# Second mixer of a two-block network: rotary partners moved by transfers and GpSimd, and its score work in another order

## The chip, the cores and the metric

The kernel runs on one core of one Trainium2 chip. The metric is device time in microseconds of one execution; the median of three runs of the kernel before is 993.6 us (989.09 to 994.18). Five engines run their own instruction lists and meet at semaphores: TensorE (PE; its weight loads are PEld), VectorE (DVE), ScalarE (ACT), GpSimd (POOL) and SyncE (SP), which here only issues transfers. All data is float32; a product of weights and activations is made from a rounded upper part and a remainder (`whi`, `wlo`), so each weight block has to be split before it is used.

## The reference, cut to what matters

Two transformer-like blocks run one after the other on 256 tokens of width 1024. The change touches the mixer of the second block only:

```python
proj = h @ w_in[l]                      # 1024 -> 2304 columns, 18 groups of 128
qa, ka, va, qd, kd, vd = jnp.split(proj, splits, axis=-1)
qa = apply_rope(qa, cos, sin)           # 8 heads of 64; likewise ka (2), qd (8), kd (8)
# apply_rope: x1, x2 = halves of a head's 64 columns
#   [x1 * c - x2 * s, x2 * c + x1 * s]
out_a = sliding_window_sink_attention(qa, ka, va, sinks[l])      # "swa"
od = differential_attention(qd, kd, vd, lam)    # softmax(0) - lam * softmax(1), times vd
out_b = rms_norm_2(od, g_diff[l]) * (1.0 - lam_init)
x = x + jnp.concatenate([out_a, out_b], axis=-1) @ w_out[l]
```

## The kernel before, in words

Weights come in units of 128 x 1024 numbers (512 KB). SP loads a unit into one of three `raw` buffers, ACT rounds it into `whi` (L1179) and DVE subtracts to get `wlo` (L1694), both rings of six. `load` waits for the `wlo` of the unit three before (`lo_ready`), and both splits wait until PE has used the unit six before (`unit_used`). `split_to(i + LEAD + 1)` at the head of each step of ACT's and DVE's loops keeps the splits four units ahead of PE.

The mixer's projection is 18 units, one group of 128 columns each, in the order `COLS2`; PE makes a unit with 24 matmuls (`a_unit_summed`) in PSUM bank 4, 5 or 6 in turn. Columns lie on partitions, so a head's two rotary halves are two quarters of 32 partitions. For a rotated group (13 of the 18: groups 0 to 4 and 6 to 13) ACT copies the four quarters crosswise out of PSUM (L1532, four instructions), DVE multiplies the bank by the cosines (`RT[0]`, L2248, which frees the bank: `q_sum`), the swapped copy by the sines (L2249), and adds (L2252: `rope_done`). Value groups (5 and 14 to 17) are copied (L2242), turned by PE (L1000) and evacuated by ACT (L1546).

The twelve jobs of the softmax are numbered by `ORDER`: 0 to 5 belong to the differential heads, 6 to 11 to swa. `scores(p)` on PE makes jobs 2p and 2p+1, at a fixed place between units. `maxima(k)` (DVE L2194, then L2204 or L2197 and two small ones) masks and takes maxima, `exponents(k)` (ACT L1512) follows, `invert_sums(k)` (DVE) divides; for each pair of differential jobs it also subtracts the second map (L2222, L2227: `p_ready`). `turn(k)` on PE transposes a group of four blocks (L980), `turned(k)` on ACT evacuates it (L1521). Nine such groups exist: 0 to 2 differential, 3 to 8 swa.

After the units PE multiplies the differential maps by the values. ACT then squares the result and takes a root (L1559, L1564), DVE inverts and scales (L2269, L2272), PE transposes (L1047), ACT and DVE write the product's two parts (L1569, L1739), and the output projection starts on them: 8 units of the `w_out` loop, the first four on the differential half. Between those run the swa product (48 matmuls of 128x64), its scaling, and its transposes (L1077); the last four output units follow. The order is all written out by hand; no scheduler changes it.

## Time and profile before

| what | us |
|---|---|
| median of three runs | 993.6 |
| lowest, highest | 989.09, 994.18 |
| the profiled execution's own time | 990.36 |
| its span in the profile | 988.6 |
| mixer, first projection unit to first product of the differential maps | 614.69 to 683.68 |
| from there to the first output unit | 683.68 to 694.84 |
| from there to the fifth output unit | 694.84 to 715.36 |
| busy over the span: PE, DVE, ACT, POOL | 939.6, 663.3, 557.0, 20.8 |

The start times are those of the first matmul of each part in PE's timeline. A matmul's end is modelled, so PE's busy share overstates how much of the time it needs; how long a piece of work takes is better read as the difference between two start times. Idle time of an engine counts only where PE waits for it in the end.

### The profile page before, as it was taken

What the parts mean: (1) busy time and instruction counts of PE and PEld (TensorE: products, weight loads), DVE (VectorE), ACT (ScalarE), POOL (GpSimd) and SP (SyncE); (2) the same over time, 40 slices, a digit from 0 to 9 for tenths busy, and PEclk for the clock granted to TensorE, in tenths of its full rate; (3) what the DMA queues carried; (4) which work ended last, traced back from release to release, by engine and by line L of the source; (5) the groups of instructions that cost most, each with busy time, mean ns of one, the idle gap of its engine ahead of it and who ended that gap; (6) DMA issues with size and microseconds to landing.
All of it is one profiled execution on the core that took longest, in us unless ns stands there. A gap on an engine that the chain in (4) does not pass through costs nothing. (4 is left out here: it accounts for less than half of the span.)

```text
span 988.6 us, 17818 instructions
## 1 busy us (share of the span) xinstructions
PE 939.6 (95%) x6292; PEld 811.4 (82%) x6292; DVE 663.3 (67%) x1097; ACT 557.0 (56%) x1018; POOL 20.8 (2%) x47
## 2 busy tenths in 40 slices
PE   6999999989989999999999999987888999999997
PEld 5788888889989877888888887977777888888885
DVE  4776666567776467766667886788367366666665
ACT  6565555477545337555555676887566346454442
POOL 3002000000000001000000000000000000000000
PEclk9999999999999999999999999999999999999999
DMA  7677666545210226765666665542156236665652
GB/s 216 204 223 222 205 183 186 164 128 151 86 66 4 65 88 166 214 187 185 186 184 198 198 174 167 171 127 88 43 149 192 61 116 197 189 202 172 198 182 85
DMA packets 204241, 153.75 MB, mean 156 GB/s; under 512 B 5323, under 2 KB 189872, under 8 KB 204192
## 3 DMA queue, kind: packets, MB, share of 16 engines
q1 hardware_dynamic: 202896, 151.08, 50.7%
q0 software_dynamic: 1296, 2.01, 0.9%
q8 instruction: 32, 0.52, 0.2%
q14 instruction: 17, 0.14, 0.0%
HBM read 152.02 MB, written 1.05 MB: 155 GB/s over the span
## 5 line engine op out<-in xcount | busy, mean ns | idle before, releaser
L474 PE MATMUL ps<-XT,whi 128*128 128x512 f32 (+1 forms) x1728 | 521.1, 363 | 7.1 <-DVE XT L1739 7.1
L1694 DVE TENSOR_TENSOR wlo<-raw,whi 128x1024 fp32r<-128x1024 f32 x280 | 336.6, 1221 | 105.8 <-ACT whi L1179 82.6
L474 PE MATMUL ps<-XT,wlo 128*128 128x256 f32 x1440 | 405.6, 282 | 0.0
L474 PEld LDWEIGHTS ps<-XT,whi 128*128 128x128 f32 x1728 | 307.5, 190 | 64.2 <-issue 7.6
L1179 ACT ACTIVATE whi<-raw 128x1024 fp32r<-128x1024 f32 x280 | 291.8, 1054 | 52.3 <-PE ps L474 12.2
L474 PEld LDWEIGHTS ps<-XT,wlo 128*128 128x128 f32 x1440 | 273.9, 190 | 2.8
L474 PE MATMUL ps<-whi,H 128*128 128x512 f32 x608 | 177.7, 393 | 1.9 <-issue 1.6
L474 PEld LDWEIGHTS ps<-whi,H 128*128 128x128 f32 x608 | 108.9, 188 | 25.0 <-issue 1.8
L474 PE MATMUL ps<-wlo,H 128*128 128x512 f32 x304 | 95.6, 392 | 0.0
L474 PE MATMUL ps<-arena 64*64 64x64 f32 (+6 forms) x1512 | 87.9, 245 | 6.3 <-ACT arena L1374 1.7
L474 PEld LDWEIGHTS ps<-arena 64*64 64x64 f32 (+3 forms) x1512 | 80.3, 150 | 13.0 <-issue 2.3
L474 PEld LDWEIGHTS ps<-wlo,H 128*128 128x128 f32 x304 | 57.1, 188 | 13.3
L474 PE MATMUL ps<-whi,XT 128*128 128x512 f32 x192 | 56.9, 401 | 1.5 <-DVE XT L1738 0.8
L1241 ACT ACTIVATE arena<-ps 128x256 f32<-128x256 f32 x44 | 16.7, 380 | 57.6 <-PE ps L474 57.6
L1251 ACT ACTIVATE arena<-ps 128x256 f32<-128x256 f32 x44 | 16.9, 383 | 50.6 <-PE ps L474 50.6
L474 PEld LDWEIGHTS ps<-whi,XT 128*128 128x128 f32 x192 | 35.2, 188 | 10.5 <-issue 2.5
L1259 ACT ACTIVATE H<-arena 128x256 fp32r<-128x256 f32 x44 | 18.4, 418 | 38.5 <-DVE arena L1839 38.5
L1635 ACT ACTIVATE arena<-ps 128x256 f32<-128x256 f32 x32 | 12.2, 382 | 46.8 <-PE ps L474 46.7
L1828 DVE TENSOR_TENSOR arena<-ps,arena 128x256 f32<-128x256 f32 x44 | 18.6, 422 | 27.6 <-ACT arena L1241 27.5
L1842 DVE TENSOR_TENSOR H<-arena,H 128x256 fp32r<-128x256 f32 x44 | 18.7, 426 | 24.4 <-ACT H L1259 24.4
L1639 ACT ACTIVATE H<-arena 128x256 fp32r<-128x256 f32 x32 | 13.4, 418 | 35.0 <-DVE arena L2357 35.0
L1739 DVE SCALAR_TENSOR_TENSOR XT<-ps,VEC,XT 128x256 fp32r<-128x256 f32 x60 | 24.3, 475 | 10.6 <-ACT XT L1216 6.9
(259 smaller groups left out, 704.3 us busy)
## 6 DMA issues: line engine op xcount, KB each, us to landing
raw<-in_ffn_w_gate SPq DMA_DIRECT2D x44, 512.0 KB, 4.3
raw<-in_ffn_w_up SPq DMA_DIRECT2D x44, 512.0 KB, 3.7
raw<-in_ffn_w_down SPq DMA_DIRECT2D x44, 512.0 KB, 4.5
raw<-in_w_in SPq DMA_DIRECT2D x36, 512.0 KB, 3.8
raw<-in_w_up SPq DMA_DIRECT2D x32, 512.0 KB, 4.0
raw<-in_w_down SPq DMA_DIRECT2D x32, 512.0 KB, 4.5
raw<-in_w_out SPq DMA_DIRECT2D x16, 512.0 KB, 3.5
raw<-in_w_ckv SPq DMA_DIRECT2D x16, 512.0 KB, 4.4
```

The source lines that it names most:

```text
L474: return pe.matmul(o, st, mv, start=start, stop=stop, skip_group_check=True)
L1179: act.activation(whi[:, n % RING, :], raw[:, n % RAW, :], ACT.Copy).then_inc(hi_ready, 1)
L1241: act.activation(GL[:, q, :], PS[4 + q][:, T:2 * T], ACT.Copy).then_inc(g_low, 1)
L1251: act.activation(UL[:, q, :], PS[6 + q][:, T:2 * T], ACT.Copy).then_inc(u_low, 1)
L1259: act.activation(H[:, q, 0:T], HS[:, q, :], ACT.Copy).then_inc(h_hi, 1)
L1635: act.activation(UL[:, q, :], PS[4 + q][:, T:2 * T], ACT.Copy).then_inc(r_low, 1)
L1639: act.activation(H[:, q, 0:T], HS[:, q, :], ACT.Copy).then_inc(r_hi, 1)
L1694: dve.tensor_tensor(wlo[:, n % RING, :], raw[:, n % RAW, :], whi[:, n % RING, :].bitcast(F32), sub).then_inc(lo_ready, 1)
L1739: return dve.scalar_tensor_tensor(XT[:, c, T:2 * T], ps, scale, hi, mul, sub)
L1828: dve.tensor_tensor(GS[:, q, :], PS[4 + q][:, 0:T], GL[:, q, :], add).then_inc(g_raw, 1)
L1842: dve.tensor_tensor(H[:, q, T:2 * T], HS[:, q, :], H[:, q, 0:T].bitcast(F32), sub).then_inc(h_ready, 1)
```

## The change

1. Rotary partners. ACT copies the bank once, unswapped (`QCP`). SP then issues four transfers of 32 x 256 numbers (32 KB each) that write the quarters crosswise into `SWP`, in a new function `partners`, called ahead of the load eight units on. DVE keeps the cosine product alone. GpSimd makes the sine product and the sum (`RSW` lies in `LWG`).
2. Order of the units: the differential heads' query and key groups are interleaved and come first, then their values, then swa's key, its queries, its values.
3. The score work: `scores(0)` to `scores(3)` stand after units 5, 9, 10 and 16 (before: 7, 9, 11, 13), `scores(4)` and `scores(5)` behind the differential product; maxima, exponents, inversions and turns are placed by tables. The swa turns 3 to 8 now stand between the output units 0 to 3, two ahead of each of the units 1 and 2 and two behind unit 2.
4. PSUM banks are given out anew to fit.

```diff
--- before.py
+++ after.py
@@ -272,6 +272,8 @@
         SWP = CLOW
+        QCP = ar(24064, 2, T)
+        RSW = LWG[:, 0:T]
...
@@ -366,7 +369,7 @@
-        VALUES = (13, 14, 15, 16, 17)
+        VALUES = (8, 9, 10, 11, 17)
@@ -377,9 +380,15 @@
         ORDER = [6, 7, 8, 9, 10, 11, 0, 2, 1, 3, 4, 5]
-        COLS2 = [6, 7, 8, 9, 10, 11, 12, 13, 0, 1, 2, 3, 4, 5, 14, 15, 16, 17]
+        COLS2 = [6, 10, 7, 11, 8, 12, 9, 13, 14, 15, 16, 17, 4, 0, 1, 2, 3, 5]
+        ROPED = [i for i, k in enumerate(COLS2) if k < 5 or 6 <= k < 14]
         OUT2_ROWS = (4, 5, 6, 7, 0, 1, 2, 3)
-        U_BANKS, TURN_BANKS = (4, 5, 6), (7, 7, 7, 3, 3, 4, 5, 4, 5)
+        U_BANKS, TURN_BANKS = (4, 5, 6), (7, 7, 7, 4, 5, 6, 7, 4, 5)
+        SC_BANKS = (0, 1, 2, 0, 1, 2, 0, 1, 4, 5, 6, 7)
+        SCORES_AT, TURN_AT = {5: (0,), 9: (1,), 10: (2,), 16: (3,)}, {10: 0, 14: 1, 16: 2}
+        MAX_AT = {5: 0, 6: 1, 9: 2, 10: 3, 11: 4, 12: 5, 16: 6, 17: 7}
...
+        INVERT_AT = {7: 0, 8: 1, 11: 2, 12: 3, 13: 4, 14: 5}
@@ -440,10 +449,24 @@
+            def partners(i):
...
+                r = ROPED.index(i)
+                sp.wait_ge(q_copy, r + 1)
+                if r >= 2:
+                    sp.wait_ge(rope_sin, r - 1)
+                for a, b in ((0, 1), (1, 0), (2, 3), (3, 2)):
+                    sp.dma_start(SWP[QUADRANTS[a], r % 2, :], QCP[QUADRANTS[b], r % 2, :]).then_inc(swp_in[r % 2], 16)
             for i, k in enumerate(COLS2):
+                partners(i - LEAD - RAW - 1)
                 load(B_WIN2 + i, 0, cols("w_in_2", k * P))
             for i, c in enumerate(OUT2_ROWS):
+                partners(N_WIN2 + i - LEAD - RAW - 1)
                 load(B_WOUT2 + i, 0, rows("w_out_2")[:, c:c + 1, :])
+            partners(N_WIN2 + KC - LEAD - RAW - 1)
@@ -941,9 +964,14 @@
-                    for k in (2 * p, 2 * p + 1):
-                        if k >= 3:
-                            pe.wait_ge(sc_sum, k - 2)
+                    if p in (1, 2):
+                        pe.wait_ge(sc_sum, 2 * p - 1)
+                    elif p == 3:
+                        pe.wait_ge(sc_sum, 5)
+                    elif p == 4:
+                        pe.wait_ge(q_sum, N_WIN2)
+                    elif p == 5:
+                        pe.wait_ge(vt_ev, 5)
...
@@ -969,12 +997,10 @@
                         pe.wait_ge(sc_exp, 6 + k - 3 + 1)
-                        if k == 3:
-                            pe.wait_ge(vt_ev, 5)
-                        elif k in (5, 6):
-                            pe.wait_ge(od_norm, k - 4)
+                        if k < 7:
+                            pe.wait_ge(sc_sum, 6 + k)
                         else:
-                            pe.wait_ge(pt_ev, k if k == 4 else k - 1)
+                            pe.wait_ge(pt_ev, k - 3)
@@ -985,52 +1011,17 @@
+                def turn_value(i, n, bank):
+                    pe.wait_ge(q_sum, i + 1)
+                    for tt in range(NT):
+                        last = pe.transpose(PS[bank][:, tt * P:(tt + 1) * P], QKV[:, COLS2[i], tt * P:(tt + 1) * P], ident)
+                    last.then_inc(vt_mm, 1)
...
-                    if i == 7:
-                        pe.wait_ge(rope_done, 6)
-                        scores(0)
-                    if i == 9:
-                        pe.wait_ge(rope_done, 8)
-                        scores(1)
-                    if i == 11:
-                        scores(2)
-                    if i == 13:
-                        pe.wait_ge(rope_done, 13)
-                        pe.wait_ge(ksw_ready, 1)
-                        scores(3)
-                    if i in (15, 17):
-                        scores(i // 2 - 3)
-                    if i in (12, 14, 16):
-                        turn(i // 2 - 6)
...
+                for i in range(N_WIN2):
+                    if i >= 3:
+                        pe.wait_ge(q_sum, i - 2)
+                    a_unit_summed(B_WIN2 + i, PS[U_BANKS[i % 3]], None if i else "mix2")
+                    if i - 1 in VALUES:
+                        n = VALUES.index(i - 1)
+                        if n:
+                            pe.wait_ge(vt_ev, n)
+                        turn_value(i - 1, n, 3)
+                    if i in SCORES_AT:
+                        pe.wait_ge(rope_done, {5: 4, 9: 8, 10: 8, 16: 11}[i])
+                        if i == 16:
+                            pe.wait_ge(ksw_ready, 1)
+                        scores(SCORES_AT[i][0])
+                    if i in TURN_AT:
+                        turn(TURN_AT[i])
...
+                pe.wait_ge(sc_sum, 6)
+                pe.wait_ge(vt_ev, 4)
+                pe.wait_ge(pt_ev, 3)
+                diff_out(0)
+                turn_value(N_WIN2 - 1, 4, 7)
+                diff_out(1)
+                pe.wait_ge(rope_done, 13)
+                scores(4)
+                scores(5)
...
+                pe.wait_ge(sc_sum, 8)
+                output(0, start=True)
+                turn(3)
+                turn(4)
+                output(1)
                 turn(5)
                 turn(6)
-                pe.wait_ge(sc_sum, 12)
-                pe.wait_ge(pt_ev, 5)
-                output(0, start=True)
+                output(2)
                 turn(7)
                 turn(8)
-                output(1)
-                output(2)
@@ -1520,61 +1546,68 @@
...
-                        if i not in VALUES:
-                            act.wait_ge(unit_used, B_WIN2 + i + 1)
-                            if n_rope >= 2:
-                                act.wait_ge(rope_done, n_rope - 1)
-                            for a, b in ((0, 1), (1, 0), (2, 3), (3, 2)):
-                                ins = act.activation(SWP[QUADRANTS[a], n_rope % 2, :],
-                                                     PS[U_BANKS[i % 3]][QUADRANTS[b], 0:T], ACT.Copy)
-                            ins.then_inc(q_swap, 1)
...
+                for i in range(N_WIN2):
+                    split_to(B_WIN2 + i + LEAD + 1)
+                    if i in ROPED:
+                        r = ROPED.index(i)
+                        act.wait_ge(unit_used, B_WIN2 + i + 1)
+                        if r >= 2:
+                            act.wait_ge(swp_in[r % 2], 64 * (r // 2))
+                        act.activation(QCP[:, r % 2, :], PS[U_BANKS[i % 3]][:, 0:T], ACT.Copy).then_inc(q_copy, 1)
...
+                squares(0)
+                value_turned(N_WIN2 - 1, 4, 7)
+                squares(1)
                 act.wait_ge(od_ss, 2)
                 act.activation(ODS, ODS, ACT.Sqrt, scale=1.0 / P, bias=con("eps_block")).then_inc(od_std, 1)
-                turned(3)
-                turned(4)
+                exponents(7)
                 for h in range(4):
...
+                exponents(8)
+                exponents(9)
+                turned(3)
+                turned(4)
                 exponents(10)
                 exponents(11)
-                for k in range(5, 9):
-                    turned(k)
+                turned(5)
+                turned(6)
                 split_to(B_WOUT2 + RING)
+                turned(7)
+                turned(8)
@@ -2241,42 +2273,38 @@
...
-                        dve.wait_ge(q_swap, n_rope + 1)
-                        dve.wait_ge(own_dve, own.n)
-                        if n_rope:
-                            dve.wait_ge(rope_done, n_rope)
-                        dve.tensor_tensor(RT[:, 0, :], bank[:, 0:T], RC, mul).then_inc(q_sum, 1)
-                        dve.tensor_tensor(RT[:, 1, :], SWP[:, n_rope % 2, :], RSN, mul).then_inc(own_dve, own.next())
-                        dve.wait_ge(q_sum, i + 1)
-                        dve.wait_ge(own_dve, own.n)
-                        dve.tensor_tensor(QKV[:, k, :], RT[:, 0, :], RT[:, 1, :], add).then_inc(rope_done, 1)
-                        n_rope += 1
+                        r = ROPED.index(i)
+                        dve.wait_ge(q_copy, r + 1)
+                        if r == 0:
+                            dve.wait_ge(own_dve, own.n)
+                        if r >= 2:
+                            dve.wait_ge(rope_done, r - 1)
+                        dve.tensor_tensor(RT[:, r % 2, :], bank[:, 0:T], RC, mul).then_inc(q_sum, 1)
...
-                    if i >= 8:
-                        maxima(i - 8)
-                    if i >= 10:
-                        invert_sums(i - 10)
-                maxima(10)
-                invert_sums(8)
-                maxima(11)
-                invert_sums(9)
+                    if i in MAX_AT:
+                        maxima(MAX_AT[i])
+                    if i in INVERT_AT:
+                        invert_sums(INVERT_AT[i])
+                maxima(8)
...
-                invert_sums(10)
-                invert_sums(11)
+                for k in range(9, 12):
+                    maxima(k)
+                for k in range(6, 12):
+                    invert_sums(k)
@@ -2442,6 +2470,15 @@
+            for r, i in enumerate(ROPED):
+                pool.wait_ge(swp_in[r % 2], 64 * (r // 2 + 1))
+                pool.wait_ge(q_sum, i + 1)
+                if r:
+                    pool.wait_ge(rope_done, r)
+                pool.tensor_tensor(RSW, SWP[:, r % 2, :], RSN, ALU.mult).then_inc(rope_sin, 1)
+                pool.wait_ge(rope_sin, r + 1)
+                pool.tensor_tensor(QKV[:, COLS2[i], :], RT[:, r % 2, :], RSW, ALU.add).then_inc(rope_done, 1)
```

DVE at the projection units 7 and 8, before (units 5 and 6 read like unit 7; `arena` is the buffer in which `RT`, `SWP`, `QKV` and the scores lie; each L2248 stands for one rotated unit):

```order
L1694 TENSOR_TENSOR wlo<-raw,whi 128x1024 [waits unit_used,hi_ready]
L2248 TENSOR_TENSOR arena<-ps,arena 128x256 [waits rope_done,own_dve,q_swap]
L2249 TENSOR_TENSOR arena<-arena 128x256
L2252 TENSOR_TENSOR arena<-arena 128x256 [waits own_dve,q_sum]
L1694 TENSOR_TENSOR wlo<-raw,whi 128x1024 [waits unit_used,hi_ready]
L2248 TENSOR_TENSOR arena<-ps,arena 128x256 [waits rope_done,own_dve,q_swap]
L2249 TENSOR_TENSOR arena<-arena 128x256
L2252 TENSOR_TENSOR arena<-arena 128x256 [waits own_dve,q_sum]
L2194 SCALAR_TENSOR_TENSOR arena<-ps,CON 128x512 [waits sc_mm]
L2204 TENSOR_REDUCE arena<-arena 128x2 [waits sc_sum]
```

DVE at units 5 and 6 now, the first two with scores:

```order
L1727 TENSOR_TENSOR wlo<-raw,whi 128x1024 [waits unit_used,hi_ready]
L2282 TENSOR_TENSOR arena<-ps,arena 128x256 [waits rope_done,q_copy]
L2227 SCALAR_TENSOR_TENSOR arena<-ps,CON 128x512 [waits sc_mm]
L2237 TENSOR_REDUCE arena<-arena 128x2 [waits sc_sum]
L1727 TENSOR_TENSOR wlo<-raw,whi 128x1024 [waits unit_used,hi_ready]
L2282 TENSOR_TENSOR arena<-ps,arena 128x256 [waits rope_done,q_copy]
L2227 SCALAR_TENSOR_TENSOR arena<-ps,CON 128x512 [waits sc_mm]
L2237 TENSOR_REDUCE arena<-arena 128x2 [waits sc_sum]
L1727 TENSOR_TENSOR wlo<-raw,whi 128x1024 [waits unit_used,hi_ready]
```

L2282 is the cosine product that was L2248; the two instructions behind it are gone, and the scores' maxima (L2227, L2237) stand in the steps of units 5 and 6 and no longer in those of 8 and 9.

What took their place stands on GpSimd's list, once per rotated unit:

```order
L2478 ISA
L2478 TENSOR_TENSOR LWG<-arena 128x256 [waits q_sum,swp_in0]
L2480 TENSOR_TENSOR arena<-arena,LWG 128x256 [waits rope_sin]
L2478 TENSOR_TENSOR LWG<-arena 128x256 [waits rope_done,q_sum,swp_in1]
L2480 TENSOR_TENSOR arena<-arena,LWG 128x256 [waits rope_sin]
```

and on SP's list, where the weight loads were alone:

```order
L403 DMA raw<-in_w_in 128x8x128 [waits lo_ready] x8
L461 DMA arena<-arena 32x256 [waits q_copy]
L461 DMA arena<-arena 32x256 x3
L403 DMA raw<-in_w_in 128x8x128 [waits lo_ready]
L461 DMA arena<-arena 32x256 [waits q_copy]
L461 DMA arena<-arena 32x256 x3
L403 DMA raw<-in_w_in 128x8x128 [waits lo_ready]
```

(On SP's list `L403` is a weight load, `L461` the transfers of one unit.) Each sine product waits for the four transfers (`swp_in0` or `swp_in1`) and for the sum before it; each set of transfers stands behind a weight load that waits for `lo_ready`.

PE behind the last projection unit, before (the rows of L474 are scores(5) and then the differential product, L1000 the last value group, L980 turns 3 and 4, L1047 the transposes for the output):

```order
L474 MATMUL ps<-arena 128x128 [waits sc_sum]
L474 MATMUL ps<-arena 128x128 x7
L1000 MATMUL ps<-CON,arena 128x128 [waits vt_ev,q_sum]
L1000 MATMUL ps<-CON,arena 128x128
L474 MATMUL ps<-arena 128x128 [waits pt_ev,vt_ev]
L474 MATMUL ps<-arena 128x128 x11
L980 MATMUL ps<-CON,arena 128x128 [waits vt_ev,sc_exp]
L980 MATMUL ps<-CON,arena 128x128 x3
L980 MATMUL ps<-CON,arena 128x128 [waits pt_ev,sc_exp]
L980 MATMUL ps<-CON,arena 128x128 x3
L1047 MATMUL ps<-CON,arena 128x128 [waits od_norm]
```

and now (L497 is first the differential product of one token half, then, behind L1018, of the other; the four rows from `128x256` on are scores(4) and scores(5)):

```order
L497 MATMUL ps<-arena 128x128 [waits pt_ev,vt_ev,sc_sum]
L497 MATMUL ps<-arena 128x128 x3
L1018 MATMUL ps<-CON,arena 128x128 [waits q_sum]
L1018 MATMUL ps<-CON,arena 128x128
L497 MATMUL ps<-arena 128x128 x8
L497 MATMUL ps<-arena 128x256 [waits q_sum,rope_done]
L497 MATMUL ps<-arena 128x256 x3
L497 MATMUL ps<-arena 128x128 [waits vt_ev]
L497 MATMUL ps<-arena 128x128 x7
L1072 MATMUL ps<-CON,arena 128x128 [waits od_norm]
L1072 MATMUL ps<-CON,arena 128x128
```

Scores(4) and scores(5) have moved from the units to behind the product, and turns 3 and 4 from here to behind the first output unit.

## Rows read from the trace of the kernel before

**Rows 1.** The page: span, busy time of each engine.

```profile
span 988.6 us, 17818 instructions
...
PE 939.6 (95%) x6292; PEld 811.4 (82%) x6292; DVE 663.3 (67%) x1097; ACT 557.0 (56%) x1018; POOL 20.8 (2%) x47
```

**Rows 2.** Busy time by stage: from:to, length, then each engine's busy us (instructions), clock.

```profile
614.69:683.68 68.99, 62.95 (x518) 59.29 (x518) 60.82 (x124) 56.32 (x138) 0.00 (x0) 1.00 0.43 135
683.68:694.84 11.16, 7.42 (x48) 7.00 (x49) 7.17 (x22) 8.89 (x30) 0.00 (x0) 0.85 0.05 20
694.84:715.36 20.52, 18.59 (x113) 15.94 (x113) 4.97 (x11) 8.64 (x30) 0.00 (x0) 1.00 0.17 52
```

**Rows 3.** PE's timeline: start us, us, what [idle before <-releaser].

```profile
614.69 0.47 PE L474 MATMUL ps<-XT,whi 128*128 128x256 f32 x2 [0.84 <-DVE XT L1739]
...
617.76 0.40 PE L474 MATMUL ps<-XT,whi 128*128 128x256 f32 x2
...
638.00 1.14 PE L474 MATMUL ps<-arena 64*128 64x256 f32 x8
639.07 0.51 PE L474 MATMUL ps<-XT,whi 128*128 128x256 f32 x2
...
645.85 1.14 PE L474 MATMUL ps<-arena 64*128 64x256 f32 x8 [0.76 <-DVE arena L2194]
...
660.00 0.66 PE L980 MATMUL ps<-CON,arena 128*128 128x128 f32 x4 [2.09 <-DVE arena L2227]
...
668.48 0.66 PE L980 MATMUL ps<-CON,arena 128*128 128x128 f32 x4 [0.59 <-DVE arena L2227]
...
683.68 1.49 PE L474 MATMUL ps<-arena 128*128 128x128 f32 x11 [1.17 <-ACT arena L1546]
...
686.46 0.60 PE L980 MATMUL ps<-CON,arena 128*128 128x128 f32 x4
690.05 1.05 PE L980 MATMUL ps<-CON,arena 128*128 128x128 f32 x4 [2.98 <-ACT arena L1521]
...
694.84 0.70 PE L474 MATMUL ps<-whi,XT 128*128 128x512 f32 x2 [0.75 <-DVE XT L1739]
...
699.00 1.11 PE L980 MATMUL ps<-CON,arena 128*128 128x128 f32 x8 [1.16 <-ACT arena L1521]
...
705.42 5.47 PE L474 MATMUL ps<-arena 128*128 128x64 f32 x48
...
715.36 0.73 PE L474 MATMUL ps<-whi,XT 128*128 128x512 f32 x2 [0.77 <-DVE XT L1738]
```

**Rows 4.** DVE's groups by line in the mixer, 614 to 727 us: busy us, mean ns.

```profile
L1694 DVE TENSOR_TENSOR wlo<-raw,whi 128x1024 fp32r<-128x1024 f32 x25 | 30.2, 1217 | 9.1 <-ACT whi L1179 9.0
...
L2252 DVE TENSOR_TENSOR arena<-arena 128x256 f32<-128x256 f32 x13 | 5.5, 425 | 1.3
...
L2249 DVE TENSOR_TENSOR arena<-arena 128x256 f32<-128x256 f32 x13 | 5.4, 415 | 0.0
```

**Rows 5.** DVE's timeline: the split ahead of the first rotated unit.

```profile
617.55 1.21 DVE L1694 TENSOR_TENSOR wlo<-raw,whi 128x1024 fp32r<-128x1024 f32 x1
```

**Rows 6.** ACT's groups by line in the mixer, same columns.

```profile
L1532 ACT ACTIVATE arena<-ps 32x256 f32<-32x256 f32 x52 | 19.5, 376 | 5.8 <-PE ps L474 5.2
```

**Rows 7.** ACT's timeline behind the differential product.

```profile
687.83 1.28 ACT L1564 ACT_TABLE_LOAD   x1
...
691.99 1.69 ACT L1569 ACTIVATE XT<-ps,SMALL 128x256 fp32r<-128x256 f32 x4 [0.26 <-PE ps L1047]
```

**Rows 8.** DMA in 614 to 638 us: traffic by slices, issues, us to landing.

```profile
raw<-in_w_in SPq DMA_DIRECT2D x7, 512.0 KB, 3.7
```

**Rows 9.** DMA issues of the whole span, smallest SP transfer with a landing.

```profile
CON<-in_consts SPq DMA_DIRECT2D x1, 65.5 KB, 1.9
```

**Rows 10.** POOL's timeline: its writes without an input, as before.

```profile
0.79 0.20 POOL L2404 MEMSET SMALL<- 128x128 f32 x1
...
94.59 0.52 POOL L2432 MEMSET LWG<- 32x512 f32 x1
```

103 lines of the change are left out of this document (42 added, 61 removed).

## The prediction

> **What bounds the kernel now.** I read the page first: PE is busy 95% of the span, DVE 67%, ACT 56%, POOL 2% [rows 1]. So only what PE waits for can be won, and the question is how much PE waits in the stage that the change touches. The busy time by stage answers that [rows 2]: from the first projection unit to the differential product PE is busy 62.95 of 68.99 us; from there to the first output unit 7.42 of 11.16; from there to the fifth output unit 18.59 of 20.52. That is 11.7 us of 100.67 in which PE stands, and nothing else of the 988.6 us of the span is touched. In the first of these stages DVE is busy 60.82 of 68.99 us: it is the second engine there.
>
> PE's timeline says which wait is last each time [rows 3]. Among the units: scores wait for DVE to have emptied a score bank (0.76 us, once more the same), the first turn waits 2.09 us for the subtracted maps, the two others 0.59 and 0.58 us. Then the differential product waits 1.17 us for ACT's evacuation of the last value group, a turn waits 2.98 us behind it, the first output unit 0.75, the turns behind that 1.16, the fifth output unit 0.77. All but the last two come from DVE and ACT being late with rotation and softmax.
>
> **What the change takes off DVE and ACT.** DVE loses two of its three instructions per rotated unit, 26 in all: 5.4 + 5.5 us [rows 4]. ACT loses 52 quarter copies, 19.5 us [rows 6], and gets 13 copies of the whole bank. An ACT copy of 32 x 256 takes 376 ns; the same length of row on 128 partitions I take at 380 ns, 5 us together, so 14.5 us go. None of this is a gain by itself: it is what lets the five waits among the units end sooner. With the differential groups first, their scores start two units earlier, and each turn stands at least two units behind the scores whose maps it needs; I count 0.76 + 0.76 + 2.09 + 0.59 + 0.58 = 4.8 us and the 1.17 as gone. What is late next are the rotations themselves.
>
> **The new time of the stage, without waits on the rotation.** Four pieces, as differences of start times in [rows 3].
> - Units: 68.99 us, less the 5.95 of waits, is 63.0. Scores(4) and (5) leave it (638.00 to 639.07 is 1.07 for a pair; the last pair with narrow blocks I take at 1.25), and the last value group's turn with them (0.4). That leaves 60.3.
> - Differential product: 683.68 to 686.46, 2.8, plus 0.3 for the value turn now between its halves: 3.1.
> - From its end to the first output unit: 686.46 to 694.84, 8.4. This is a chain of ACT, DVE and PE (squares, table load at 687.83, root, scaling, transposes, the two parts from 691.99 [rows 7]), not PE's work. Turns 3 and 4 leave its shadow and scores(4) and (5) enter it: about 2.3 us of PE's work inside 8.4, hidden. ACT gets `exponents(7)` between the root and the two parts, with the table load that used to stand later; both end about when the transposes do. So 8.4 stays. If that cover is gone, it costs up to 1 us.
> - First to fifth output unit: 20.5. A pair of turns takes 699.00 to 700.11, 1.1 us; two pairs come in, 2.2. Of the 1.16 us wait in front of turn 7 I take back about half, since `turned(8)`, which the swa product needs, now stands behind two weight splits on ACT. I add up 21.8.
>
> Together 93.6 us against 100.7: 7.1 us less. PE's work is the same to the instruction, so this is all from waits; what stays is the chain of 8.4.
>
> **The new wait.** A rotation was four ACT copies and three DVE instructions in a row. Now it is an ACT copy of 0.4 us, four transfers and two GpSimd instructions.
> - Transfers. SP issues them behind the weight load of seven units on, on the same queue. That load is released by DVE's split, 617.55 + 1.21 for the first unit [rows 5], in steady state just about when the unit ends; it takes 3.7 us to land [rows 8]. If the 128 KB must queue behind it, they land some 0.6 us after it, 4.3 us behind the unit; if they do not queue, 0.5 + 1.9 us, from the small SP transfer of the trace [rows 9], is 2.4. I take 4.3, since they share a queue.
> - GpSimd. The trace shows no instruction of it with an input. Its writes of 128 and 512 columns take 0.20 and 0.52 us [rows 10], 0.3 for 256 columns: lower end. DVE's sum takes 0.43; three passes of GpSimd's rate (two reads, one write) and two starts give 0.9 to 1.2: upper end. I take 0.7 each, the middle, and 0.2 for each semaphore: 1.8 for both. Two lower ends and two semaphores are 1.0, two upper ends 2.8.
> - So a rotation ends 6.1 us behind its unit, 3.3 at the very best, 7.5 at the worst of these.
>
> Three places wait for one. Scores(0), behind unit 5, needs unit 3: 2 units of 2.89 us ((638.00 - 617.76) / 7 [rows 3]), 5.8 us. Scores(1), behind unit 9, needs unit 7: 5.8 plus a value turn, 6.1. Scores(3), behind unit 16, needs unit 14: again 5.8, but there DVE is late. In the steps of units 12 to 14 it has maxima, inversions and subtractions on top of the split, and the load of seven units on, with the transfers behind it on SP, starts about 1.4 us after the end of unit 14. Waits of 0.7 (the first rotation starts late, because the split at 617.55 does), 0.4 and 1.3 us, and 0.1 for each restart: 2.7 us.
>
> A second effect comes on top. The split reads two SBUF operands and takes 1.22 us [rows 4]; it begins about 4.4 us behind a unit, when the transfers land. If GpSimd and DVE get in each other's way there, each of the three waits grows by 0.7 to 0.9 us. The trace has no moment with both engines at work, so it says neither yes nor no. I take a bit under half: 0.9 us for all three. New waits 3.6 us, net gain 7.1 - 3.6 = 3.5 us.
>
> The page SBUF — State Buffer of the Trainium skill, section Who interferes with whom, speaks against the change here: a VectorE instruction with two SBUF inputs and a GpSimd instruction that reads SBUF exclude each other for their whole length. Taken at its word it puts about 2.4 us on the three waits and makes the gain about 2 us; taken as absent the gain is about 4.4. No row here shows it. The page GPSIMD Engine Reference of the Trainium skill, section 3.1 Elementwise — side-by-side cycle accounting, gives about 2.6 cycles for an element of a two-input instruction; by it one of ours is an estimated 0.55 us plus dispatch, which would leave the sum as it is.
>
> **Against which time.** The profiled execution took 990.36 us, 1.8 beyond its span; 3.5 less is 986.9. The median of the runs shown is 3.2 above it, and 3.5 below the median is 990.1. Runs of this kernel scatter by 5 us (989.09 to 994.18), and the next median can fall at either end. I say 989.3, between the two and nearer to the median. Within 0.5% of 993.6 us (5.0 us) a measurement of this kernel can hardly tell a change from none.
>
> **The rivals.**
> 1. The rotation is hidden. If the transfers do not queue behind the load (2.4 instead of 4.3 us) or GpSimd needs 0.3 us an instruction, rotations end before they are asked for; only the late DVE at unit 14 can cost up to 1 us. Gain 6 to 7 us: 987. For it: queue traffic is moderate, 7 loads in 24 us [rows 8]. Against: all is on SP's queue.
> 2. A wait takes the place of the one removed. With 1.2 us per GpSimd instruction and full exclusion with DVE's split, the three waits are about 2.2 + 1.9 + 2.8 us, 7 in all: gain 0, 993. For it: DVE's 60.82 of 68.99 us, in which a hold-up spreads. Against: DVE loses 10.9 us of that.
> 3. Slower: the rotation becomes a loop that sets the pace. DVE's product of unit i waits for the sum of unit i-2, its split stands behind, the load behind the split, the transfers of the next unit behind the load. Three units' time, 8.65 us, must cover 0.35 + 1.22 + 0.1 + transfers + GpSimd. It decides once transfers and GpSimd take over 7.0 us (I have 6.1 with the wait in it). Each further us stretches a unit by 0.33, over 13 rotated units 4.3 us, and each of the three waits by 1: 7.3 us per us. At 8.3 us, the gain of 7.1 is used up and about 5 more are lost: 998. For it: no number of mine holds a transfer within SBUF. Against: it needs both unknown prices at their upper ends.
>
> **How the numbers follow.** Forecast (gain 2 to 6 us) 0.45, rival 1 0.23, rival 2 0.19, rival 3 0.13. Rival 1 is faster by over 0.5%; of the forecast's own case about a third ends beyond 5 us, by its upper end and by scatter: 0.38 faster. Rival 3 and a little of rival 2 are slower: 0.14. The rest, 0.48, is the same. The range is 984 to 997: below it only a full rival 1 at the low end of the scatter, above it the outer half of rival 3. The forecast's own range is 986.5 to 992.
>
> **What would show it.** Right: 26 GpSimd instructions of 0.6 to 0.9 us; transfers landing about with the load ahead of them; PE's waits on GpSimd of 0.5 to 2 us in front of scores(0), (1) and (3); no wait in front of turns 0 to 2; first output unit about 8.4 us behind the differential product, and the fifth 21 to 22 us behind the first. Wrong: splits of DVE that grow well over 1.22 us or start late, units that come further apart than 2.9 us (rival 3), scores without a wait (rival 1), or a longer chain between product and output, for which I have taken nothing.

## The result, and the profile after

The changed kernel is slower: median 1001.4 us (999.45 to 1004.17, four runs) against 991.4 us (986.72 to 994.18, the three runs of before and a fourth of 986.72); ratio 1.0112, 95% interval 1.0087 to 1.0138. I had forecast 989.3 with a range up to 997. The profiled execution took 1000.59 us. The page of the kernel after, its span, engines and granted clock, to be held against [rows 1]:

```profile
span 998.8 us, 17839 instructions
...
PE 945.6 (95%) x6292; PEld 816.9 (82%) x6292; DVE 656.6 (66%) x1071; ACT 542.0 (54%) x979; POOL 43.9 (4%) x73
...
PEclk9999999999999999999999999898899999999999
```

DVE and ACT have less to do and GpSimd more, as the change promised; PE has 6 us more with the same 6292 matmuls. Matmuls do not grow by themselves, so the row of the clock is the first hint. The same three stages as in [rows 2], with the granted clock as the third number from the end:

```profile
615.23:691.72 76.49, 65.91 (x493) 62.80 (x494) 48.62 (x82) 37.70 (x87) 22.37 (x26) 0.89 0.47 140
691.72:702.58 10.86, 6.32 (x61) 5.47 (x59) 6.91 (x17) 9.37 (x35) 0.68 (x1) 0.91 0.14 48
702.58:726.71 24.13, 22.62 (x129) 19.33 (x129) 10.59 (x31) 10.64 (x36) 0.00 (x0) 0.90 0.15 44
```

Together 111.5 us against 100.7: 10.8 us more, which covers the whole difference (the spans differ by 10.2). PE's timeline says where it stands; the rows answer to [rows 3]:

```profile
636.85 2.08 PE L497 MATMUL ps<-arena 64*128 64x256 f32 x8 [3.99 <-POOL arena L2480]
...
655.32 1.26 PE L497 MATMUL ps<-arena 64*128 64x256 f32 x8 [2.85 <-POOL arena L2480]
...
684.74 2.08 PE L497 MATMUL ps<-arena 64*128 64x256 f32 x8 [3.73 <-POOL arena L2480]
...
702.58 1.19 PE L497 MATMUL ps<-whi,XT 128*128 128x512 f32 x2 [2.53 <-issue]
```

The three waits that I had named are there, in front of scores(0), (1) and (3), and nowhere else among the units: 10.6 us where I had 3.6. And the eight matmuls behind the first and third take 2.08 us, where [rows 3] has 1.14. Stretches cut at these waits show why (columns as above, the third number from the end is the clock):

```profile
632.90:636.80 3.90, 0.00 (x0) 0.00 (x0) 1.56 (x2) 1.97 (x3) 2.77 (x4) 0.86 0.71 210
636.85:638.90 2.05, 2.05 (x9) 1.23 (x9) 0.42 (x1) 0.00 (x0) 1.18 (x2) 0.50 0.65 178
638.90:642.00 3.10, 3.10 (x16) 3.10 (x15) 2.51 (x3) 0.00 (x0) 0.94 (x2) 0.50 0.34 97
...
643.00:652.40 9.40, 9.40 (x80) 9.23 (x78) 6.76 (x13) 5.57 (x13) 1.48 (x2) 1.00 0.54 153
...
702.58:706.98 4.40, 4.40 (x10) 3.44 (x11) 4.16 (x10) 1.19 (x5) 0.00 (x0) 0.50 0.01 2
```

Near the end of the first wait the clock falls to 0.50 (1.2 GHz; it is 0.50 from 636.00 to 636.85), and it comes back only after more than 5 us of work, likewise behind the third wait. Behind the second it falls only after PE has begun again (1.00 from 655.3 to 656.0, 0.50 from 656.5) and is back some 4 us after that start. Full-speed time lost behind the three waits, as length times (1 - clock): 2.85, 1.7 and 2.8 us, 7.35 in all, and 2.2 us in the first output unit. That last part does not come from the transfers: it stands behind a wait of 2.53 us for the differential chain, and e1 and e6 below, which have no transfers, have it too (clock 0.50 and 0.54 there).

What makes the rotation late stands in the chain of waits of that stretch, from the transfers of the first rotated unit to scores(0) (start, length, what):

```profile
619.75 0.61 SPq L461
...
621.67 2.54 DMA arena<-arena
...
624.29 1.80 POOL LWG L2478
...
626.16 0.74 POOL arena L2480
...
627.00 0.42 DVE arena L2282
...
628.41 1.42 DVE wlo L1727
...
629.85 0.37 SPq L403
...
630.32 0.53 SPq L461
...
632.17 2.48 DMA arena<-arena
...
634.72 1.28 POOL LWG L2478
...
636.07 0.73 POOL arena L2480
```

Read from the top: four transfers of unit 0, GpSimd's two instructions, DVE's cosine product of unit 2 (it waits for the sum of unit 0), DVE's split, SP's load released by it, the transfers of unit 3, GpSimd again. From sum to sum that is 9.9 us for three units. Unit 3's own ACT copy began at 627.20, so its rotation ended 9.6 us behind the unit where I had 6.1. GpSimd's share of this is 2.1 us (I had 1.8), the rest is the time until the transfers have landed. In front of scores(3) the sine product itself was long, beside a split of DVE:

```profile
682.08 1.81 POOL L2478 TENSOR_TENSOR LWG<-arena 128x256 f32<-128x256 f32 x1 [1.52 <-DMA arena<-arena]
```

SP's issues, by source line:

```profile
L461 SPq DMA_DIRECT2D arena<-arena x52: 507/590/615, 619.8 to 687.2; - x52
...
DMA to landing us min/median/max: 1.8/2.7/4.1
```

Each transfer holds SP for 0.59 us, a set of four for 2.4 to 2.5 us.

### The profile page after: what moved, and what is told of

Read it like the earlier page. It is cut to its first block, busy times and chain, and to the rows that moved or that the text cites. A ratio compares the mean times of both kernels' runs of the same rounds, so it can differ in the third digit from the quotient of the medians.

```text
span 998.8 us, 17839 instructions
## 1 busy us (share of the span) xinstructions
PE 945.6 (95%) x6292; PEld 816.9 (82%) x6292; DVE 656.6 (66%) x1071; ACT 542.0 (54%) x979; POOL 43.9 (4%) x73
## 3 DMA queue, kind: packets, MB, share of 16 engines
HBM read 152.02 MB, written 1.05 MB: 153 GB/s over the span
## 4 chain that ended last, share of the span: by engine, by line
PE 77%; DVE 8%; ACT 6%; DMA 4%; issue 3%; SPq 1%; POOL 1%; DVEq 0%; ACTq 0%
PE ps L497 76%; DVE wlo L1727 3%; ACT whi L1205 2%; DMA arena<-arena 1%; DMA raw<-in_w_co 1%; SPq L461 1%; DMA raw<-in_w_ckv 1%; DVE XT L1772 1%; DMA raw<-in_ffn_w_gate 1%; POOL LWG L2478 1%; ACT arena L1226 1%; DMA raw<-in_w_up 0%; ACT arena L1538 0%; ACT XT L1242 0%; DMA raw<-in_ffn_w_up 0%
## 5 line engine op out<-in xcount | busy, mean ns | idle before, releaser
L497 PE MATMUL ps<-XT,whi 128*128 128x512 f32 (+1 forms) x1728 | 525.0, 366 | 7.4 <-DVE XT L1772 7.4
L497 PE MATMUL ps<-XT,wlo 128*128 128x256 f32 x1440 | 407.4, 283 | 0.0
L497 PEld LDWEIGHTS ps<-XT,whi 128*128 128x128 f32 x1728 | 311.1, 192 | 64.1 <-issue 8.1
L497 PEld LDWEIGHTS ps<-XT,wlo 128*128 128x128 f32 x1440 | 275.8, 192 | 2.8
L497 PE MATMUL ps<-whi,H 128*128 128x512 f32 x608 | 177.7, 393 | 2.2 <-issue 1.5
L497 PEld LDWEIGHTS ps<-whi,H 128*128 128x128 f32 x608 | 108.9, 188 | 25.3 <-issue 1.8
L497 PE MATMUL ps<-arena 64*64 64x64 f32 (+6 forms) x1512 | 89.7, 248 | 14.9 <-POOL arena L2480 10.6
L497 PEld LDWEIGHTS ps<-arena 64*64 64x64 f32 (+3 forms) x1512 | 81.3, 152 | 21.9 <-POOL arena L2480 11.2
L497 PE MATMUL ps<-wlo,H 128*128 128x512 f32 x304 | 95.6, 392 | 0.0
L497 PEld LDWEIGHTS ps<-wlo,H 128*128 128x128 f32 x304 | 57.1, 188 | 13.3
L497 PE MATMUL ps<-whi,XT 128*128 128x512 f32 x192 | 58.7, 411 | 3.3 <-issue 2.5
L1267 ACT ACTIVATE arena<-ps 128x256 f32<-128x256 f32 x44 | 16.7, 380 | 58.6 <-PE ps L497 58.5
L497 PEld LDWEIGHTS ps<-whi,XT 128*128 128x128 f32 x192 | 36.2, 194 | 12.6 <-issue 4.3
L497 PE MATMUL ps<-wlo,XT 128*128 128x512 f32 x96 | 31.6, 401 | 0.0
```

The source lines that it names most:

```text
L497: return pe.matmul(o, st, mv, start=start, stop=stop, skip_group_check=True)
L1267: act.activation(GL[:, q, :], PS[4 + q][:, T:2 * T], ACT.Copy).then_inc(g_low, 1)
```

## Experiments

Each kernel was timed against the kernel before on the same chip; ratios are to that kernel. "After" below is the changed kernel, 1001.4 us. It was not timed again beside the experiments, and the medians of the kernel before on their chips are 989.8 to 991.8 us, so a difference in us between an experiment and after is uncertain by about 2 us; where it is not clearly larger, the ratios decide.

**e1: the order alone.** ACT's quarter copies and DVE's three instructions put back.

```diff
-  act.activation(QCP[...], PS[...][:, 0:T], ACT.Copy)      # four transfers, GpSimd
+  for a, b in ((0, 1), (1, 0), (2, 3), (3, 2)):            # and DVE's sine product and sum
+      ins = act.activation(SWP[QUADRANTS[a], ...], PS[...][QUADRANTS[b], 0:T], ACT.Copy)
```

> The new order of units, scores, turns and banks, with the rotation of the kernel before (four quarter copies on ACT, three instructions on DVE, no transfers, nothing on GpSimd). Theory 1, the new rotation alone costs (its transfers make it late, and TensorE's clock falls in the waits): the order is worth most of the 7.1 us that I counted, less what the fuller ACT and DVE take back: 985 to 989 us. Theory 2, the order itself costs (scores stand too near their units, turns sit in the output stage): 996 us or more, with waits of PE in front of scores or turns again.

Measured: 989.99 us, ratio 0.9986 (0.9976 to 0.9995). Faster, but by 1.8 us, just outside the range of theory 1: the order does no harm, yet most of the gain stays away. PE's timeline of this kernel:

```profile
673.17 1.13 PE L494 MATMUL ps<-arena 64*128 64x256 f32 x8 [1.90 <-issue]
...
680.91 0.44 PE L1015 MATMUL ps<-CON,arena 128*128 128x128 f32 x2 [2.26 <-DVE arena L2274]
...
690.93 1.19 PE L494 MATMUL ps<-whi,XT 128*128 128x512 f32 x2 [2.52 <-issue]
```

With the old rotation ACT (key copies) and DVE (last value group) are late again at the end of the units (waits of 1.90 and 2.26 us), and the first output unit runs at half clock.

**e6: no transfers, GpSimd kept.** ACT's quarter copies into `SWP`, GpSimd's two instructions as in after.

> The changed kernel without transfers: ACT again makes four quarter copies out of PSUM, GpSimd keeps the sine product and the sum, order of units and scores as changed. Theory 1, the loss comes from the transfers: a rotation ends 1.5 + 1.8 = 3.3 us behind its unit, no wait on GpSimd is left in front of scores(0), (1), (3), the clock stays up, and since DVE has 0.85 us less per rotated unit than with the order alone (990.0 us) the time is 986 to 989 us. Rival, GpSimd work beside DVE's splits is what costs (exclusion between the two): waits on GpSimd of 1 us or more remain and the time is 994 us or more.

Measured: 988.91 us, ratio 0.9981 (0.9964 to 0.9998). Theory 1. This is the main comparison: with the same order, the same GpSimd instructions and DVE program, copies in place of transfers are worth 12.5 us. PE's scores(0), (1) and (3), and one of GpSimd's sums:

```profile
635.21 1.14 PE L494 MATMUL ps<-arena 64*128 64x256 f32 x8
...
648.70 1.13 PE L494 MATMUL ps<-arena 64*128 64x256 f32 x8
...
675.31 1.82 PE L494 MATMUL ps<-arena 64*128 64x256 f32 x8 [2.39 <-issue]
```

```profile
633.41 1.60 POOL L2480 TENSOR_TENSOR arena<-arena,LWG 128x256 f32<-128x256 f32 x1
```

No wait on GpSimd is left; the 2.39 us in front of scores(3) are for the key copies on ACT. Four of GpSimd's first five sums still take 1.6 us here, beside DVE's splits, so that exclusion alone costs PE no wait when the rotation starts early enough.

**e2: work for PE during the waits.**

```diff
+  if i in {5: 14, 9: 10, 16: 14}:         # ahead of scores(0), (1), (3)
+      pe.wait_ge(q_sum, i - 1)
+      for c in range(...): mm(PS[U_BANKS[(i + 1) % 3]][:, :], XT[:, c % KC, 0:P], XT[:, c % KC, :])
```

> The changed kernel, with useless matmuls of 128 x 512 (14, 9 and 14, into the bank of the next unit) in front of scores(0), scores(1) and scores(3), so that PE does not stand still while it waits for the rotation. Theory A, part of the loss is the granted clock, which in the changed kernel is at 1.2 GHz for some 5 us behind each of the three waits (the three stretches hold 7.3 us of lost full-speed time): the waits behind the filling shrink to about 1 us each, the granted clock stays at full, and the time is about 994 to 996 us. Theory B, the clock does not matter there, since the units behind a wait are held by splits and rotations anyway: 1001 us, the same as the changed kernel, and the units wait for DVE instead.

Measured: 995.43 us, ratio 1.0053 (1.0032 to 1.0074): 6 us less than after. Theory A. (The kernel has ten useless matmuls ahead of scores(1), not nine.) The scores behind the filling, and a stretch behind the first of them:

```profile
637.04 1.14 PE L497 MATMUL ps<-arena 64*128 64x256 f32 x8 [0.58 <-POOL arena L2484]
...
681.33 1.13 PE L497 MATMUL ps<-arena 64*128 64x256 f32 x8 [0.70 <-POOL arena L2484]
```

```profile
637.00:642.00 5.00, 4.96 (x40) 4.58 (x41) 3.24 (x5) 0.72 (x3) 2.33 (x4) 1.00 0.47 136
```

The rotation is no earlier (scores(0) starts 21.4 us behind the first unit, in after 21.6), but the clock stays at 1.00 and the scores take 1.14 us. So about 6 of the 12.5 us are the half clock, not the waits.

**e3 and e4: half and twice the transfers.** `((0, 1), (1, 0))` in place of all four pairs; and each transfer cut into two of 128 columns.

> The changed kernel with two of the four transfers of each rotation left out (partitions 64 to 127 are rotated with stale partners). Theory 1, SP's issue time of 0.59 us for each transfer sets when the rotation ends: SP is busy 1.2 us less for each unit, the rotation ends about 1.2 us sooner, and the waits in front of scores(0), (1) and (3) shrink from 4.0, 2.9 and 3.7 us to about 2.5, 1.5 and 2.0: about 992 us. Rival, exclusion between GpSimd and DVE or the GpSimd instructions themselves set it: the waits stay within 0.5 us and the time at 1001 us.

> The changed kernel with each transfer cut into two of half the columns: eight for each rotation, the same bytes. Theory 1, issue time on SP: 4.8 us for eight and 0.5 us for the weight load is more than a unit's 2.9 us, so the 13 rotated units come some 5.3 us apart: about 2.4 us more for each, 1030 us. Rival, the transfers' bytes or the exclusion set it: no change, 1001 us; if it is the count of transfers in the DMA engines instead of SP's issue, landing from issue grows well over 2.7 us while SP's issue rows stay short.

Measured: e3 998.9 us, ratio 1.0064 (1.0049 to 1.0079), 2.5 us less than after by the medians and 4.8 by the ratios; the three waits sum to 8.7 us. e4 1023.34 us, ratio 1.0316 (1.0301 to 1.0331). SP's timeline of e4:

```profile
621.04 5.05 SPq L462 DMA_DIRECT2D arena<-arena  x8
626.13 0.58 SPq L403 DMA_DIRECT2D raw<-in_w_in  x1
626.76 6.11 SPq L462 DMA_DIRECT2D arena<-arena  x8
```

A set of eight and a load hold SP for 5.7 us at least, more than a unit's 2.9: SP is the bound, and the same bytes cost 22 us more, less than my 29 but by the same mechanism. Below that bound, in e3, a quarter to a half of what I expected comes back: the transfers' median from issue to landing rises to 3.4 us (why was not tested; a whole load is issued right beside them), and three of the first four sums on GpSimd take 1.6 us. So the issue time is one part of the latency, and the landing another.

**e7, e10, e13, e9: what the landing waits for.** e7: four buffers for `QCP`, `SWP` and `RT` in place of two. e10: e7 with two of the four transfers issued by ACT. e13: ACT issues the weight loads of units 7 and on, SP the transfers alone. e9: those loads move an eighth of their bytes.

> The changed kernel with four buffers in place of two for the bank copy, the swapped copy and the cosine product. Theory 1, the two-deep loop (cosine product waits for the sum two before, copy waits for the transfers two before; 7.8 us of waits on DVE and 7.8 on ACT) makes splits, loads and so transfers late: these waits go, the three waits of scores shrink from 10.6 us to about 5 in all, and the time is about 995 us. Rival, only the latency of a single rotation counts (issue, landing, GpSimd): the scores' waits stay above 9 us and the time at 1001 us.

> Four buffers, and two of the four transfers of each rotation issued by ACT on its own queue right behind its copy, the other two by SP as before. Theory 1, issue time on SP and the place behind the load make the transfers late: ACT's transfers land about 2 us after the copy, SP's set takes 1.2 instead of 2.45 us, and the time falls below that of the four-deep kernel, to 990 to 993 us. Rival, ACT becomes the bound (1.05 split, 0.38 copy and 1.2 of issuing are 2.65 of a unit's 2.9 us): late rounded parts of the weights hold PE, and the time is above that of the four-deep kernel.

> The changed kernel, in which ACT issues the weight loads of units 7 and on (behind its bank copy), so that SP has only the transfers. Theory 1, the place on SP behind a load that waits for DVE's split is what makes the transfers late: they are issued right behind the copy, the first sine product starts some 5 us behind it at every rotation (5.8 to 7.5 in the changed kernel), the scores' waits fall from 10.6 us to about 3 in all, and the time to 993 to 995 us. Rival, four transfers beside a load take that long in the DMA engines whoever issues them: GpSimd starts 6 us or more behind the copy, waits stay above 7 us, 1000 us.

> The changed kernel, in which 11 weight loads of the projection (units 7 to 17) move an eighth of their bytes (64 KB; the rest of the unit keeps stale numbers). Issues, semaphores and instructions stay. Theory 1, the transfers queue behind the bytes of the weight load: they land 1.8 us after their issue instead of 2.7 to 4.1, rotations end some 2 us sooner, the scores' waits fall from 10.6 us to about 4 in all and the time to about 994 us. Rival, SP's issue time and the two-deep loop set it: the waits stay above 8 us, the time at 999 to 1001 us.

| | us | ratio (95%) | waits of scores(0), (1), (3) | landing, median |
|---|---|---|---|---|
| after | 1001.4 | 1.0112 (1.0087 to 1.0138) | 3.99, 2.85, 3.73 | 2.7 |
| e7 | 1001.31 | 1.0101 (1.0073 to 1.0129) | 3.45, 2.86, 3.08 | 2.8 |
| e10 | 1003.56 | 1.0109 (1.0075 to 1.0144) | 3.74, 2.20, 3.69 | 3.5 (SP), 2.3 (ACT) |
| e13 | 998.95 | 1.0101 (1.0070 to 1.0132) | 3.90, 2.31, 4.02 | 3.3 |
| e9 | 995.46 | 1.0052 (1.0033 to 1.0070) | 2.62, 1.05, 3.75 | 2.1 |

e7 refutes the theory that the two-deep loop is the cause: cut there, SP's own pace (0.6 + 2.5 us per unit against 2.9) takes its place, and unit 3's rotation still ends 9.1 us behind it. e13 shows that the place on SP is not the main cause. The first unit's transfers leave right behind the copy, yet GpSimd's sine product starts 5.95 us behind it (5.8 in after). For unit 3 it is 6.5 us in place of 7.5, but the copy comes 0.6 us later, since ACT issues the loads, and the sum takes 1.58 us beside a split: the wait of scores(0) stays. Four buffers together with the loads off SP were not tried. Fewer bytes in the loads (e9, 5.9 us less) do help: the sine products of units 0 and 3 start 5.1 and 6.7 us behind their copies, and the first two waits shrink. Its scores(3) waits as before, for the loads beside the transfers of unit 14 are those of `w_out`, which e9 leaves whole; so e9 says nothing of that wait. By their ratios e7, e10 and e13 cannot be told from after; only e9 can. The landing rows of e9 and of e13, where loads and transfers have different queues:

```profile
DMA to landing us min/median/max: 1.8/2.1/3.3
```

```profile
DMA to landing us min/median/max: 1.8/3.3/4.7
```

1.8 us is the shortest from issue to landing in all of these; with whole loads, in after, e7 and e13, the medians are 2.7 to 3.3 us and the longest 4.0 to 4.7, whichever queue the loads are on. e10 showed ACT's share landing sooner (2.3 us), but ACT's issuing delayed its own copies (unit 3's by 0.8 us).

**e8: GpSimd beside DVE, in the kernel before.** 26 useless instructions of the rotation's shape, each pair started by DVE's cosine product.

```diff
+  pool.wait_ge(q_sum, i + 1)
...
+  pool.tensor_tensor(ar(24064, T), RC, RSN, ALU.mult).then_inc(idle_done, 1)
...
+  pool.tensor_tensor(ar(24320, T), ar(24064, T), RSN, ALU.add).then_inc(idle_done, 1)
```

> The kernel before, with 26 useless GpSimd instructions of the rotation's shape (two for each rotated unit, 128 x 256, started when DVE's cosine product of the unit is done; nobody waits for them until the end of the units). Theory 1, GpSimd and DVE's instructions with two SBUF inputs exclude each other: several of the 26 instructions take 1.1 to 1.8 us instead of 0.73 us, each of them beside a DVE split, and DVE's splits or its sine products of that stretch grow or start late; with DVE busy 61 of 69 us there the time grows by 2 to 6 us, to 993 to 997 us. Rival, the long GpSimd instructions of the changed kernel had another cause (its fresh transfers): all 26 stay near 0.73 us and the time at 991 us.

Measured: 996.06 us, ratio 1.0060 (1.0040 to 1.0081). DVE and GpSimd in that kernel:

```profile
621.30 0.78 DVE L2252 TENSOR_TENSOR arena<-arena 128x256 f32<-128x256 f32 x1
622.00 1.76 DVE L1694 TENSOR_TENSOR wlo<-raw,whi 128x1024 fp32r<-128x1024 f32 x1
```

```profile
620.95 0.85 POOL L2450 TENSOR_TENSOR arena<-arena 128x256 f32<-128x256 f32 x1 [243.79 <-DVE arena L2248]
621.88 0.80 POOL L2452 TENSOR_TENSOR arena<-arena 128x256 f32<-128x256 f32 x1
```

The time is as theory 1 has it, but the other engine pays: DVE's 0.43 us instruction takes 0.78 (all 13 of them 758 to 780 ns), since it starts inside GpSimd's first; the split takes 1.76 in place of 1.22, since it starts inside the second. GpSimd came first and stays at 0.80 to 0.85. In after it is the other way round where DVE's split came first: the sine product at 624.29 takes 1.79 us beside the split at 624.26. That is what the Trainium skill says on the page SBUF — State Buffer, section Who interferes with whom: an exclusive lock, and whoever issues first holds it. The traces agree: in both cases the later one ends about its own length (0.43, 1.22 or 0.73 us) behind the end of the earlier one, within 0.2 us.

**e15: scores(0), (1), (2) one unit later.**

```diff
-  SCORES_AT, TURN_AT = {5: (0,), 9: (1,), 10: (2,), 16: (3,)}, {10: 0, 14: 1, 16: 2}
+  SCORES_AT, TURN_AT = {6: (0,), 10: (1,), 11: (2,), 16: (3,)}, {11: 0, 15: 1, 16: 2}
...
```

> The changed kernel with scores(0), (1) and (2) one unit later (after units 6, 10 and 11) and their maxima, exponents, inversions and first two turns with them. Theory 1, a rotation that ends 8 to 10 us behind its unit costs only through the place where it is asked for: the waits of 4.0 and 2.9 us in front of scores(0) and (1) fall to about 1 and 0, the half clock behind them (4.4 us of lost time) goes too, and the time is 991 to 993 us. Rival, the loop of rotation, split, load and transfers sets the pace of the units, so that a wait comes back elsewhere (units, or scores(3) above 3.7 us): 998 us or more.

Measured: 990.26 us, ratio 0.9995 (0.9979 to 1.0010): 11.1 us less than after, with all transfers as they were. PE's timeline:

```profile
638.01 1.14 PE L497 MATMUL ps<-arena 64*128 64x256 f32 x8 [0.86 <-POOL arena L2480]
...
676.86 1.14 PE L497 MATMUL ps<-arena 64*128 64x256 f32 x8 [4.02 <-POOL arena L2480]
```

The first two waits are nearly gone (0.86 us and none), scores(3) waits as long as in after (4.0 us), and nothing comes back in the units. So the late rotation is no loop that paces PE; it costs where PE asks too early. The units' stage is 66.18 us, 10.3 us shorter than in after.

**e11, e12, e14, e16, e17: the rest of the counted gain.** All have useless matmuls of 128x512 around the differential transposes (8 and 10), to keep PE at work ahead of the first output unit. e11 is after with these alone; e12 is e6 and e14 is e1 with these and the key copies one step earlier; e16 is e15 and e17 is e6 with these and scores(3) after unit 17.

> The changed kernel with useless matmuls of 128 x 512 only around the differential transposes: 8 ahead of them, 10 behind them and ahead of the first output unit. Theory 1, of the 24.1 us from the first to the fifth output unit some 2.4 us are TensorE at 1.2 GHz behind the two idle stretches in front of the first output unit: that unit takes 2.8 instead of 5.2 us, the clock stays up, and the time is 2 to 2.5 us below the changed kernel: about 999 us. Rival, the stage is held by the chain on ACT and DVE (turns, exponents): the first unit gets shorter and the wait appears in front of turn 3 or the swa product, no change in time, 1001 us.

> Quarter copies on ACT, rotation's sum on GpSimd, no transfers (988.9 us alone), with two more edits: the swapped key copies of swa stand one step earlier on ACT (after unit 14 instead of 15), which should take 2.4 us of wait in front of scores(3) and some 1.5 us of half clock behind it; and the useless matmuls around the differential transposes. Theory 1: about 2.5 us from each, 984 to 985 us, faster than both kernels. Rival, the scores' wait has another releaser (the last sum on GpSimd or DVE) and the clock's 2.4 us are hidden behind ACT: 988 to 989 us.

> The new order with the rotation of the kernel before (990.0 us), the swapped key copies one step earlier on ACT, and the useless matmuls around the differential transposes. Nothing runs on GpSimd and no transfers. Theory 1, the order leaves two idle stretches that cost a half clock (1.9 us of wait in front of scores(3) with 1.5 us behind it, 2.4 us in the first output unit): 985 to 987 us, below both kernels. Rival, these stretches are filled only in name, since ACT and DVE are what the stage waits for with the old rotation: the wait moves to the last value group and the differential chain, 989 to 990 us.

> The kernel of e15 (990.3 us) with scores(3) after unit 17 in place of 16 (its maxima and exponents later to match) and the useless matmuls around the differential transposes. Theory 1, each place where PE asks for a rotation less than 8 to 10 us behind its unit has its own price: the 4.0 us wait in front of scores(3) goes, the first output unit runs at full clock (1.7 us less in e11), and up to 1 us comes back because exponents stand later: 984 to 986 us, below both kernels. Rival, ACT and DVE take the place (the later maxima and exponents hold the turns between the output units): 988 us or more.

> The kernel of e6 (ACT's quarter copies, GpSimd's rotation, no transfers, 988.9 us) with scores(3) after unit 17 and the useless matmuls around the differential transposes. Theory 1, the 2.4 us wait in front of scores(3), the half clock behind it and that in the first output unit go: 984 to 986 us. Rival, as with the earlier key copies and the same matmuls (988.2 us), the wait comes back in front of the last value group's turn, since DVE is late there: 987 to 989 us.

| | us | ratio (95%) |
|---|---|---|
| e11 | 999.69 | 1.0092 (1.0066 to 1.0118) |
| e12 | 988.21 | 0.9984 (0.9964 to 1.0004) |
| e14 | 989.40 | 0.9991 (0.9973 to 1.0009) |
| e16 | 988.34 | 0.9988 (0.9966 to 1.0011) |
| e17 | 988.18 | 0.9971 (0.9953 to 0.9988) |

In e11 the stage from the first to the fifth output unit is 21.93 us at clock 1.00, against 24.13 at 0.90: 2.2 us, and 1.7 in the medians. In e12 and e14 the rival held: a wait on DVE's copy of the last value group comes up (2.4 and 3.3 us). In e16 and e17 one comes up in front of turn 2, for DVE's subtraction (2.85 and 1.99 us). e17 is the one of these whose interval lies below 1, by 0.3%; the earlier hopes of 984 to 986 us held only for single executions. The stages of e16's profiled one (986.18 us) add up to 97.05 us, 3.6 below before:

```profile
617.06:681.75 64.69, 60.24 (x498) 57.90 (x499) 48.33 (x80) 36.88 (x82) 22.10 (x24) 1.00 0.56 166
681.75:692.17 10.42, 9.86 (x73) 8.09 (x71) 7.66 (x20) 9.47 (x36) 1.45 (x2) 1.00 0.15 52
692.17:714.11 21.94, 20.43 (x129) 17.73 (x128) 10.66 (x31) 11.83 (x42) 0.00 (x0) 1.00 0.16 49
```

Its medians show only 1.6 us of it, within the scatter (984.61 to 997.73). What makes that scatter was not settled; one candidate stands at the end.

## Why the prediction was wrong

- **The order's gain, 7.1 us.** Right in size by subtraction, but no run shows the whole of it. Take the 10.6 us of waits and the 7.35 us of clock out of the 76.49 us of units: 58.5, where I had 60.3. Product to first output unit took 10.9 (I had 11.5), first to fifth 24.1 less 2.2 of clock, 21.9 (I had 21.8). No wait stands in front of turns 0 to 2. (My own terms for this last piece, 20.5 + 2.2 less half of 1.16, add up to 22.1, not 21.8.) What the runs gave is far less: 1.8 us with the old rotation (e1), 2.3 with GpSimd's and without transfers (e6). With the old rotation ACT and DVE are late again; and in e6 the key copies on ACT and the half clock in the first output unit are left.
- **Transfers, 4.3 us behind the unit: this step failed.** I had 0.1 us for SP (in rival 3 it stands as such), and weighed only whether the bytes queue behind the load. Measured: 0.59 us for each issue, so that a set holds SP for 2.4 to 2.5 us and its last issue starts 1.8 to 1.9 us behind its first, and 1.8 to 4.1 us from there to landing. The sine product starts 5.8 us behind the copy for the first unit and 7.5 for unit 3, which also waits behind the previous set and a load held by DVE's split. Even my "3.3 at the very best" for the whole rotation was too low (its terms, 2.4 + 1.0, give 3.4, and those of "7.5 at the worst", 4.3 + 2.8, give 7.1): 1.9 us to the fourth issue and 1.8 us to land are 3.7 us without GpSimd. The trace of before showed single issues of 0.37 us for loads; I never multiplied it by four.
- **GpSimd, 0.7 us an instruction.** Right: 0.73 us undisturbed.
- **Exclusion, 0.9 us for all three waits.** It exists, and I had it too small: the last sine products in front of scores(0), (1) and (3) took 1.27, 0.85 and 1.81 us, together 1.7 us more than 0.73 each, and the first rotation's 1.1 us more. That it costs PE is shown in e8 and that it need not is shown in e6; its share of the 10.6 us was not measured alone.
- **Waits, 3.6 us.** 10.6 us. The subtraction itself holds up: the rotations that the three scores need ended 9.6, 8.7 and 9.8 us behind the start of their copy; less the 5.8, 6.1 and 5.8 us that I had counted to the scores this gives 3.8, 2.6 and 4.0, and 3.99, 2.85 and 3.73 were measured. Only the latency put into it was wrong.
- **Restarts, 0.1 us each: this failed too.** TensorE at half clock behind a wait of 2.9 to 4.0 us costs 1.7 to 2.9 us, 7.35 in all, and 2.2 us more go in the first output unit; [rows 2] had the sign of it (clock 0.85 in the stage with the 2.98 us wait) and I did not use it. e2 got back 6 us of the 7.35, e11 about 2 of the 2.2.
- **Rival 3** named the right places and the right loop, and gave 998. But the loop is not what costs: e7 breaks it and gains nothing, e15 leaves it and gains 11 us. Its price of 7.3 us per us of latency, 4.3 of it in the pace of the units, does not describe what happened; that its 998 is nearer than my 989.3 is luck.

In sum, waits 7.0 us above mine and clock 9.5 us that I had at nearly nothing, less 2.3 us of gains that came out larger: 14.2 us, from 97.2 to the 111.5 measured.

## What to carry to other kernels

Count a set of transfers between partitions as issue time for each one on its queue (0.59 us here), plus the shortest landing (1.8 us), plus what loads under way beside it add (0.9 to 1.5 us in the median), and place its reader by that sum: here one unit further away took 11 of their 12.5 us off the time. Each microsecond of PE's waits cost another 0.7 us in clock here (7.35 on 10.6), so when a wait cannot be removed, look for work to put into it or in front of it. And four quarter copies on an engine with room for them (1.5 us) beat four small transfers (5.8 to 7.5 us until their reader starts) where the latency counts, as here.

## What the hardware showed that I had not expected

- SBUF to SBUF transfers of 32 KB: 0.51 to 0.62 us of issue each in after, 1.8 us at least from issue to landing. Half the bytes change neither (e4's 16 KB transfers: 0.59 and 1.8 us).
- The clock can fall while PE works. In e17, behind an idle time of only 0.74 us that e16 has too, it dropped during the swa product (48 matmuls of 64 columns) and stayed down for some 10 us, so that product took 8.26 us; in e16 the same 48 took 5.57:

```profile
703.35:706.00 2.65, 2.65 (x23) 2.65 (x24) 0.28 (x1) 0.00 (x0) 0.00 (x0) 0.97 0.79 231
706.00:709.00 3.00, 3.00 (x16) 3.00 (x16) 0.70 (x2) 0.00 (x0) 0.00 (x0) 0.50 0.48 146
```

- After a wait the fall is not certain at once: in e15 the scores behind a 4.02 us wait still ran at 1.14 us, and the clock fell in the stretch behind them (0.53 from 677.9 to 681.0).
